# Feed-forward matmuls: each 512-column one directly followed by the 256-column one of its block, in place of rows of eight of each form

## The reference, cut to what matters

```
def swiglu(h, w_gate, w_up, w_down):
    return (jax.nn.silu(h @ w_gate) * (h @ w_up)) @ w_down
...
x = x + 0.5 * swiglu(rms_norm(x, ffn_norm[l, 0]), ffn_w_gate[l, 0], ffn_w_up[l, 0], ffn_w_down[l, 0])
```

## Time and profile before

| | us |
|---|---|
| median of 3 runs | 2378.58 |
| lowest and highest | 2377.38, 2380.64 |
| the profiled execution | 2379.08 |
| its span (first to last instruction) | 2377.3 |
| TensorE busy | 2342.5 |
| VectorE busy | 1667.2 |
| ScalarE busy | 1277.5 |

### The profile page before, as it was taken

How to read it: one execution, slowest core, us unless ns; L and a number is a source line. 1 busy time by engine, 2 the same in 40 slices (tenths; PEclk the granted TensorE clock), 3 DMA queues, 4 the chain that set the end, 5 groups by cost and what they waited for, 6 DMA issues and landing times.

```text
span 2377.3 us, 33669 instructions
## 1 busy us (share of the span) xinstructions
PE 2342.5 (99%) x14084; PEld 2054.9 (86%) x14084; DVE 1667.2 (70%) x2153; ACT 1277.5 (54%) x1587; POOL 74.4 (3%) x106
## 2 busy tenths in 40 slices
PE   8999999999999999999999999999999999999999
PEld 7889899888888978888889877888888888778888
DVE  8866755876776787767766766587677667756873
ACT  5545654554554665545555754455455467544553
POOL 2000000000000010100010000001000100000000
PEclk9999999999999999999999999999999999999999
DMA  7555445565655525666655533566555555334654
GB/s 218 183 187 175 130 125 187 185 188 185 191 184 185 163 72 174 211 188 189 194 182 178 176 123 127 165 201 208 188 187 186 187 179 168 125 125 161 193 183 136
DMA packets 347191, 409.59 MB, mean 172 GB/s; under 512 B 7878, under 2 KB 309408, under 8 KB 347040
## 3 DMA queue, kind: packets, MB, share of 16 engines
q1 hardware_dynamic: 343776, 401.66, 53.1%
q0 software_dynamic: 3072, 5.69, 0.9%
q10 hardware_dynamic: 192, 0.08, 0.0%
HBM read 406.35 MB, written 1.05 MB: 171 GB/s over the span
## 4 chain that ended last, share of the span: by engine, by line
PE 94%; DVE 3%; ACT 2%; DMA 1%; issue 1%; DVEq 0%; ACTq 0%
PE bank L591 14%; PE acc L591 12%; PE bank L1217 10%; PE bank L594 7%; PE bank L667 7%; PE acc L594 6%; PE acc L667 6%; PE acc L656 4%; PE bank L1166 4%; PE bank L670 4%; PE acc L670 3%; PE bank L1164 2%; PE acc L2522 2%; PE bank L615 1%; PE bank L3076 1%; PE bank L3113 1%
## 5 line engine op out<-in xcount | busy, mean ns | idle before, releaser
L498 DVE TENSOR_TENSOR part_lo<-raw,part_hi 128x2048 fp32r<-128x2048 f32 (+3 forms) x390 | 870.5, 2235 | 371.8 <-ACT part_hi L491 368.3
L491 ACT ACTIVATE part_hi<-raw 128x2048 fp32r<-128x2048 f32 (+3 forms) x390 | 728.8, 1869 | 320.0 <-DMA raw<-in_ffn_w 93.4
L591 PE MATMUL bank<-hT,part_hi 128*128 128x512 f32 x1408 | 353.0, 392 | 0.0
L591 PE MATMUL acc<-hT,part_hi 128*128 128x512 f32 x1280 | 321.3, 393 | 0.0
L591 PEld LDWEIGHTS bank<-hT,part_hi 128*128 128x128 f32 x1408 | 253.7, 189 | 45.8
L591 PEld LDWEIGHTS acc<-hT,part_hi 128*128 128x128 f32 x1280 | 230.1, 189 | 41.2
L1217 PE MATMUL bank<-part_hi,hT 128*128 128x512 f32 x768 | 247.5, 395 | 1.0 <-issue 1.0
L594 PEld LDWEIGHTS bank<-hT,part_lo 128*128 128x128 f32 x1408 | 192.1, 190 | 13.7
L594 PE MATMUL bank<-hT,part_lo 128*128 128x256 f32 x1408 | 196.3, 282 | 0.0
L594 PEld LDWEIGHTS acc<-hT,part_lo 128*128 128x128 f32 x1280 | 174.6, 190 | 12.5
L594 PE MATMUL acc<-hT,part_lo 128*128 128x256 f32 x1280 | 178.4, 282 | 0.0
(11 more groups left out here) (504 smaller groups left out, 3185.6 us busy)
## 6 DMA issues: line engine op xcount, KB each, us to landing
raw<-in_ffn_w SPq DMA_DIRECT2D x120, 1024.0 KB, 5.3
raw<-in_w_in SPq DMA_DIRECT2D x48, 1024.0 KB, 5.1
raw<-in_ffn_w_up SPq DMA_DIRECT2D x44, 1024.0 KB, 5.3
raw<-in_ffn_w_gate SPq DMA_DIRECT2D x43, 1024.0 KB, 5.3
raw<-in_ffn_w_down SPq DMA_DIRECT2D x32, 1024.0 KB, 5.2
raw<-in_hy_w_in SPq DMA_DIRECT2D x22, 1024.0 KB, 5.3
raw<-in_ffn_w_down SPq DMA_DIRECT2D x16, 768.0 KB, 4.8
raw<-in_ffn_w SPq DMA_DIRECT2D x16, 768.0 KB, 4.4
```

What stands on the lines that cost most here:

```text
L491: t.e.activation(part_hi[:, n % SLOTS, 0:size], raw[:, n % SLOTS, 0:size], ACT.Copy).then_inc(hi_ready, 1)
L498: t.e.tensor_tensor(part_lo[:, n % SLOTS, 0:size], raw[:, n % SLOTS, 0:size], part_hi[:, n % SLOTS, 0:size].bitcast(F32), ALU.subtract).th ...
L591: pe.matmul(b.rearrange("p (h s) -> p h s", h=2), slot_cols(s, 0)[:, k, f * P:(f + 1) * P], hT[:, :, k, :], start=(k == 0), stop=False, sk ...
```

## The change

Two loops over the contraction blocks become one, in `ffn_up` and in `ffn_down`. The 256-column matmul of a block follows directly behind the 512-column one of the same block. `ffn_up_first` and `ffn_up_opening` keep their order.

```diff
@@ ffn_up
                 for k in range(KD):
                     pe.matmul(b.rearrange("p (h s) -> p h s", h=2), slot_cols(s, 0)[:, k, f * P:(f + 1) * P],
                               hT[:, :, k, :], start=(k == 0), stop=False, skip_group_check=True)
-                for k in range(KD):
                     mm = pe.matmul(b[:, 0:S], slot_cols(s, 1)[:, k, f * P:(f + 1) * P], hT[:, 0, k, :],
                                    start=False, stop=(k == KD - 1), skip_group_check=True)
@@ ffn_down
                 for i in ks:
                     pe.matmul(out.rearrange("p (h s) -> p h s", h=2), slot_cols(s, 0)[:, i - ks.start, f * P:(f + 1) * P],
                               ff[:, :, i, :], start=(i == 0), stop=False, skip_group_check=True)
-                for i in ks:
                     mm = pe.matmul(out[:, 0:S], slot_cols(s, 1)[:, i - ks.start, f * P:(f + 1) * P], ff[:, 0, i, :],
                                    start=False, stop=(i == FF_K - 1), skip_group_check=True)
```

## The result

The changed kernel takes 2392.92 us (median of 4 runs, 2387.32 to 2393.86), the kernel before 2378.58. The ratio is 1.0058 with a 95% interval of [1.0046, 1.007]: 14 us slower, where 7 faster was forecast. The profiled execution is the fastest of the four, 2387.32 us with a span of 2385.5.

What follows compares the result with a forecast made beforehand. TensorE's feed-forward matmul distances were taken to bound the kernel: 349.2 - 347.5 = 1.7 ns, times 4096 pairs, 7.0 us off 2379.1 gives 2372.1 us (2371.6 against the median), range 2358 to 2386.

Steps and rivals of the forecast that it cites:

- What bounds the kernel: Feed-forward matmuls on TensorE: start-to-start distance alone decides; 4096 pairs at 349.2 ns, one ns a pair worth 4.1 us.
- I take 347.5 ns for an alternating pair, the place of the earlier trace: The sum's step: alternating feed-forward pairs cost what the two-by-two end of `ffn_up_first` shows, 347.5 ns.
- the 1.7 ns forecast: Saving for each feed-forward pair, 349.2 - 347.5 ns; times 4096 it gives 7.0 us.
- two by two at 352: End of `ffn_up_first` in two of seven stages, which had waited for operands shortly before: 352 ns a pair.
- The sign that the prediction named for being wrong: In the feed-forward part: 0.24 behind a wide matmul, or 0.12 and more on the mean behind a narrow one.
- No toll for each change of kind shows: Read at the end of `ffn_up_first`: changing kind every two matmuls, not every eight, adds no visible cost.
- The bounds: Cheapest and dearest readings for a feed-forward pair: 342 ns, 30 us less, and 360 ns, 44 us more.
- Nothing later takes it away: Weight transfers and VectorE keep up with feed-forward pieces 27 ns shorter, so the gain stays.
- Rival 2: Slower: every wide feed-forward matmul, behind a narrow one, pays its row's highest price; 353 ns, +15.6 us, 2394; chance 0.17.
- Rival 1: Order is indifferent in the feed-forward loops: the pair is 349.2 ns again, 2378.6 us within 5; chance 0.26.
- rival 3: More gain than forecast in the feed-forward pairs: 345 ns, 17 us less, 2361; chance 0.19.
- The range: Whole kernel from 2358 to 2386 us, taking in rivals 3 and 1 and half the way to rival 2.

Runs made afterwards that it cites:

- e16: The changed kernel unaltered, run once more: 2392.29 us, 1.0057 of the kernel before; 353.3 ns a pair, first stage too.
- e3: Against the kernel before, rows of 2: two wide, two narrow matmuls of the same two blocks in one bank; 2376.01 us, ratio 0.999.
- e1: Against the kernel before, rows of 16: wide matmuls of both output blocks, then the narrow ones of both; 2373.28 us, ratio 0.9981.
- e7: Against the kernel before, rows of 32: rows of 16, with every other piece starting with its narrow matmuls; 2371.69 us, ratio 0.9972.
- e4: Against the changed kernel, still alternating, but each narrow matmul adds into another bank than the wide ones beside it; 2392.34 us, 1.0059 of before.
- e5: Against the changed kernel, still alternating, but both matmuls have 384 columns, leaving part of the computation out; 2369.83 us, 0.9962 of before.
- e8: Against the changed kernel, only gate and up pieces alternate, down pieces keep their rows; 2387.45 us, 1.0036 of before.
- e18: Against the changed kernel, still alternating, but the narrow matmul first in each pair; 2372.87 us, 0.9977 of before.
- e13: Against the changed kernel, weight blocks of 64 columns for the wide matmuls only (not the first of each accumulation); 2346.62 us, 0.9878 of before.
- e14: Against the changed kernel, weight blocks of 64 columns for the narrow matmuls only (not the first of each accumulation); 2369.6 us, 0.9959 of before.
- e15: Against the changed kernel, alternating with 512 and 384 columns in place of 512 and 256; 2638.35 us, 1.1098 of before.
- e11: Against the kernel before, rows of 8 kept, weight blocks of 64 columns except the first of each accumulation; 2360.59 us, ratio 0.9926.

## Why the prediction was wrong, point by point

**What bounds the kernel** was right: the feed-forward matmuls don't wait, and the distance from start to start is all. The 349.2 ns, the 4096 pairs and the 4.1 us for each nanosecond held.

**The step that failed is the sum's "I take 347.5 ns for an alternating pair, the place of the earlier trace rows".** It measured 353.3 in seven of eight stages (in e16 in all eight), 5.8 more. 4.1 ns over the earlier trace rows, times 4096, is 17 us; 14 were measured. The rest is the short cheap part of each stage and what else differs between two executions: the records of e16 sum to 15.3 us more than those of before, and its span is 13.7 us longer. The place of the earlier trace rows was read rightly but for the rounding of the chain: the records give 1393 ns for its four pairs, 348.3 each in place of 347.5, and e3, with the same distances for whole stages, runs at 348.3 too. So half of the 1.7 ns forecast was rounding. The step itself fails because one by one is another order than two by two, and no row of before has it: the earlier trace rows has single wide ones, with two narrow ones between them., two by two at 352, was a warning that I put down to operands that had come late. It says that one order can have two prices, and the sum used one. The sign that the prediction named for being wrong, 0.24 behind a wide one, is what the timeline shows at 460 us.

**"No toll for each change of kind shows"** was wrong as a rule. Rows of 8 and more do pay 20 ns for each return to wide (e1, e7), rows of 2 pay 3.

**The bounds** of 342 and 360 held the 353.3. The bank, the order of high and low weights, and the down pieces' waits stood in the sum at nothing, and they do cost nothing (e4, e5, e8).

**Nothing later takes it away** can't be judged, as nothing was gained.

**Rival 2** gave 353 ns and 2394, and both came out, in part by luck. Its reason, that every wide one stands behind a narrow one and so pays the highest price of its row, did not: in the first stage, and in seven stages of e18, every wide one stands behind a narrow one and costs 230.

**Rival 1** (indifferent) is refuted by the ratio's interval, rival 3 (345 ns) by the 353.3, though e18 comes near it in its price for a pair.

**The range** ended at 2386 because rival 2 had a chance of 0.17 and was cut in half. Its place was known and two of the seven places in the trace read so; that would have been worth more.

**What stays open.** The cause: why six distances repeat as 240, 120, 236, 114, 232, 118, and what in the state ahead selects them. Known from the runs: with equal sizes it doesn't appear (e5); it doesn't hang on banks (e4) or on the order of high and low; with weight blocks of 64 columns it doesn't appear either, for the wide matmul at 340 to 342 (e13), for the narrow one at 346.7 (e14), where the load and the number of output rows were halved together; 512 and 384 columns have an extra of 13.3 (e15). No theory that I had gives all of these numbers. Each price but that of the changed kernel is read from one execution, in which all later stages agree; that another order than one by one has a second price as well is not excluded.

## What to carry to other kernels

Where TensorE is the bound as here, matmuls of one size with their loads had a fixed price, and mixing two sizes had a price that depended on the order by up to 2% (346.7 to 353.3 ns), without any wait in the list: read distances from start to start, not busy times. Where the views round to 10 ns, take them over as many matmuls as you can. Long rows of one size are the order whose price can be foreseen (e7, 2371.69, the fastest here that computes everything, with e18 at 2372.87 within its spread). A short sample of an order is not its steady price; look for a second stretch of the same order, and if the two differ, treat both as possible outcomes.

## What the runs showed of the hardware that I had not expected

- The same instructions in the same order ran at 346.7 or 353.3 ns for a pair, steadily for over 100 us, in two executions of one kernel (the first stage of the changed kernel and of e16). The two parted behind the same small matmuls, at 31.6 and 32.7 us.
- In steady rows at the full clock, 128 columns more cost 53.3 ns, and 13.3 ns came on top with a load of 128 columns (226.7, 173.3, 120.0). With a load of 64, 256 columns took 113.3 and not 120.0 (e11). The wide ones of e11 did not fall with it (224 to 236).
- The granted clock fell to half (1.2 GHz) for 3.4 us at 262.6 us in the hybrid stage of the kernel before, 1.5 us after the end of a wait of 1.47 us, with TensorE busy again by then. In the changed kernel it didn't fall behind a wait of 1.5 us at the same place.
